# A 256-row transformer chain in split float32: x turned among the last products of the stage ahead, modulation sums and gate rows moved from TensorE to DMA and VectorE

## What is computed

```python
# block A, twice (l = 0, 1)
h = h + 0.5 * rms(swiglu(rms(h), w_in, w_out))        # stages 0 and 3, inner width 2816
m = even_mixer(rms(h)) if l == 0 else odd_mixer(rms(h))  # stage 1: attention and convolution; stage 4: GLA
h = h + rms(m)
h = h + 0.5 * rms(swiglu(rms(h), w_in, w_out))        # stages 2 and 5

# block B
mod = silu(c) @ w_ada + b_ada                         # 1024 x 6144, one row
shift1, scale1, gate1, shift2, scale2, gate2 = split(mod, 6)
y = rms(x, n1) * (1 + scale1) + shift1                # stage 6: projections, attention, retention
x = x + gate1 * (merged @ w_out)
y = rms(x, n2) * (1 + scale2) + shift2                # stage 7: swiglu
x = x + gate2 * ffn(y)
out = rms(x, final)
```

## Time and profile before

| | |
|---|---|
| runs | 1500.93, 1498.14, 1501.36 us; median 1500.93 |
| profiled execution | 1501.93 us, of which the span from first to last instruction is 1500.1 us |
| TensorE matmuls | 1452.5 us busy, 97% of the span, 6819 matmuls |
| TensorE weight load | 1195.0 us, 80% |
| VectorE, ScalarE, GpSimd | 938.8 us (63%), 723.6 us (48%), 167.0 us (11%) |
| DMA | 279.15 MB, mean 186 GB/s |
| mean granted clock of TensorE | 0.991 of 2.4 GHz |

### The profile page before, as it was taken

One profiled execution on the slowest core, in us unless ns is written; L12 is line 12 of the kernel. 1 busy time (PEld: TensorE's weight loads), 2 busy tenths in 40 slices (PEclk: granted clock), 3 DMA queues, 4 the chain that ended last, 5 costly groups with the idle time before them and its releaser, 6 DMA issues.

```text
span 1500.1 us, 17986 instructions
## 1 busy us (share of the span) xinstructions
PE 1452.5 (97%) x6819; PEld 1195.0 (80%) x6819; DVE 938.8 (63%) x1291; ACT 723.6 (48%) x1058; POOL 167.0 (11%) x260
## 2 busy tenths in 40 slices
PE   7999999999999999999899999999999999899998
PEld 6888878777888878888778788887877787688886
DVE  5666556677656476664667766654568566555553
ACT  5544355465444354443644544444555634444442
POOL 1700010000000010000153100000543110000000
PEclk9999999999999999999999999999999999999999
DMA  8766745127676576565533486653745344455551
GB/s 283 246 200 228 242 151 196 36 91 260 217 236 236 187 236 220 196 250 180 191 122 120 147 269 200 216 198 105 240 140 194 129 168 169 140 183 182 170 192 74
DMA packets 201717, 279.15 MB, mean 186 GB/s; under 512 B 8804, under 2 KB 126096, under 8 KB 201632
## 3 DMA queue, kind: packets, MB, share of 16 engines
q1 hardware_dynamic: 201376, 277.90, 55.0%
q10 hardware_dynamic: 256, 0.11, 0.0%
HBM read 276.93 MB, written 1.05 MB: 185 GB/s over the span
## 4 chain that ended last, share of the span: by engine, by line
PE 92%; ACT 3%; DVE 3%; issue 2%; POOL 0%; DMA 0%; ACTq 0%; DVEq 0%; POOLq 0%
PE ps L543 28%; PE ps L546 27%; PE ps L544 27%; PE ps L828 2%; PE ps L1062 1%; DVE wlo L464 1%; PE ps L710 1%; PE ps L1342 1%; ACT whi L455 1%; PE ps L495 1%; ACT xh L742 0%; ACT xtmp L1647 0%; DVE h L697 0%; PE ps L1013 0%; PE ps L986 0%
## 5 line engine op out<-in xcount | busy, mean ns | idle before, releaser
L464 DVE TENSOR_TENSOR wlo<-raw,whi 128x1024 fp32r<-128x1024 f32 (+2 forms) x474 | 565.3, 1222 | 199.9 <-ACT whi L455 199.6
L543 PE MATMUL ps<-whi,xh 128*128 128x512 f32 (+2 forms) x1440 | 573.1, 398 | 22.6 <-ACT xh L742 14.8
L544 PE MATMUL ps<-wlo,xh 128*128 128x512 f32 (+2 forms) x1440 | 559.2, 388 | 0.0
L546 PE MATMUL ps<-whi,xl 128*128 128x512 f32 (+2 forms) x1440 | 551.7, 389 | 0.0
L455 ACT ACTIVATE whi<-raw 128x1024 fp32r<-128x1024 f32 (+2 forms) x474 | 470.8, 1043 | 155.8 <-PE ps L546 152.1
L543 PEld LDWEIGHTS ps<-whi,xh 128*128 128x128 f32 x1440 | 273.4, 190 | 83.1 <-issue 22.9
L546 PEld LDWEIGHTS ps<-whi,xl 128*128 128x128 f32 x1440 | 273.0, 190 | 56.6
L544 PEld LDWEIGHTS ps<-wlo,xh 128*128 128x128 f32 x1440 | 273.5, 190 | 51.7 <-issue 0.2
L543 PE MATMUL ps<-whi,gh 128*128 128x512 f32 x440 | 173.0, 393 | 0.0
L544 PE MATMUL ps<-wlo,gh 128*128 128x512 f32 x440 | 171.3, 389 | 0.0
L546 PE MATMUL ps<-whi,gl 128*128 128x512 f32 x440 | 153.5, 389 | 0.0
(11 more groups left out here) (242 smaller groups left out, 967.6 us busy)
## 6 DMA issues: line engine op xcount, KB each, us to landing
raw<-in_ffn_w_in_dram SPq DMA_DIRECT2D x174, 512.0 KB, 4.9
raw<-in_ffn_w_out_dram SPq DMA_DIRECT2D x40, 1024.0 KB, 5.0
raw<-in_w_in_dram SPq DMA_DIRECT2D x26, 1024.0 KB, 4.9
adat<-in_w_ada_dram SPq DMA_DIRECT2D x96, 256.0 KB, 5.3
raw<-in_w_ffn_gate_dram SPq DMA_DIRECT2D x22, 512.0 KB, 3.9
raw<-in_w_ffn_up_dram SPq DMA_DIRECT2D x22, 512.0 KB, 5.1
raw<-in_hyb_w_in_dram SPq DMA_DIRECT2D x10, 1024.0 KB, 5.1
raw<-in_gla_w_in_dram SPq DMA_DIRECT2D x10, 1024.0 KB, 5.0
```

The costliest lines, as they stand in the source:

```text
L464: e.tensor_tensor(split_of(wlo, j), raw_of(j), split_of(whi, j).bitcast(F32), ALU.subtract).then_inc(*wlo_made.up(j))
L543: e.matmul(ps[:, 0:n], a, whi_of(j, k), start=first and k == 0, stop=False)
L544: last = e.matmul(ps[:, 0:n], a, wlo_of(j, k), start=False, stop=False)
L546: last = e.matmul(ps[:, 0:n], b, whi_of(j, k), start=False, stop=final and k == subs[j][2] - 1)
```

## The change

What it does, in parts:

1. `pe_down` takes `then`: the transposes of the next stage's tok 0 stand ahead of the last held product (ahead of the last two for stages 6 and 7). `LAG` becomes 6 in stages 4 and 6 and 7 in stage 5. With `late`, one sub-tile is popped less at the end.
2. `first_order` leads with six sub-tiles of tok 0 (seven in stages 6 and 7), and `late` stands ahead of the fifth (sixth).
3. ScalarE and VectorE have another order of splits at a stage's entry; `dve_residual` and `dve_ada_x` take `between`, a split put between their two steps.
4. K's turn moves from chunk 2 to the first step of chunk 3, Q's to the third; the levels' steps move earlier or later as in the list.
5. The modulation sums leave TensorE: SP stores `adaacc` to DRAM in four DMAs, in pieces of 32 floats, and reads it back in four, turned by blocks of 32; VectorE adds twice, turns 32x32 blocks, reduces and adds the bias. The adds of tiles move by two units.
6. The gate rows leave TensorE: SP writes eight columns of `modc` to DRAM and loads them as rows to all partitions.

```diff
-        LAG = {st: 4 if st == 1 else 5 for st in range(8)}
+        LAG = {0: 5, 1: 4, 2: 5, 3: 5, 4: 6, 5: 7, 6: 6, 7: 5}
...
-                if j == last_sub[u] and ada_tile(u, -1):
-                    ada_add(e, *ada_tile(u, -1))
+                if j == last_sub[u]:
+                    if u - 1 in ada_tiles:
+                        ada_add(e, *ada_tiles[u - 1])
+                    if u in ada_summed:
+                        ada_sum(e, ada_summed[u])
...
+        def ada_sum(e, c):
+            z = fold
+            e.wait_ge(*s_fold.at(c))
+            e.tensor_tensor(z[:, 0:256], z[:, 0:256], z[:, 256:512], ALU.add).then_inc(*ada_step.up(c, 0))
+            e.wait_ge(*ada_step.at(c, 0))
+            e.tensor_tensor(z[:, 0:P], z[:, 0:P], z[:, P:256], ALU.add).then_inc(*ada_step.up(c, 1))
+            e.wait_ge(*ada_step.at(c, 1))
+            e.transpose(z[:, 256:384], z[:, 0:P]).then_inc(*ada_step.up(c, 2))
+            e.wait_ge(*ada_step.at(c, 2))
+            e.tensor_reduce(modc[:, 4 * c:4 * c + 4], z[:, 256:384].rearrange("p (b n) -> p b n", b=4), AX.X, ALU.add
+                            ).then_inc(*ada_added.up(c, 8))
...
+        def load_ada(e, u):
+            if u in ada_tiles:
+                c, k = ada_tiles[u]
+                n = 8 * c + k
+                if n >= 2:
+                    e.wait_ge(*ada_added.at(*divmod(n - 2, 8)))
+                e.dma_start(adat[n % 2][:, :], ada_view[:, k, c * 512:(c + 1) * 512]).then_inc(*s_ada[n % 2].up(n))
+            if u in ada_sent:
+                c = ada_sent[u]
+                e.wait_ge(*ada_added.at(c, 7))
+                for b in range(4):
+                    e.dma_start(ada_out[c].rearrange("p (q b n) -> b p q n", q=4, b=4)[b],
+                                adaacc[:, b * P:(b + 1) * P].rearrange("p (q n) -> p q n", q=4)).then_inc(*s_sent.up(c))
+            if u in ada_read:
+                c = ada_read[u]
+                e.wait_ge(*s_sent.at(c))
+                e.wait_ge(*(mod_made.at(c - 1) if c else vec_made.at(1)))
+                for q in range(4):
+                    e.dma_start(fold[32 * q:32 * (q + 1), :].rearrange("p (r n) -> p r n", r=4),
+                                ada_out[c, :, q * P:(q + 1) * P].rearrange("(r p) n -> p r n", r=4)
+                                ).then_inc(*s_fold.up(c))
...
-            lead = {0: 4, 6: 6, 7: 6}.get(st, 5)
+            lead = {0: 4, 6: 7, 7: 7}.get(st, 6)
...
-                if (i, tok) == ((0, 1) if st >= 6 else (3, 0)):
+                if (i, tok) == ({0: 3, 6: 5, 7: 5}.get(st, 4), 0):
                     late()
...
-                if i < len(order) - lag and not late or len(held) > lag:
+                if i < len(order) - lag and not late or late and len(held) >= lag and i < len(order) - 1:
                     one(held.pop(0), 1)
-            for i in held:
+            for k, i in enumerate(held):
+                if then and k == len(held) - then[0]:
+                    then[1]()
                 one(i, 1)
...
+            return (2, lambda: pe_ada_x(e, st, 0)) if st >= 6 else (1, lambda: pe_enter(e, st, 0))
...
                 dve_residual(e, st - 1, 0)
+                split_lo(e, j0 + 4)
                 dve_enter(e, st, 0)
-                split_lo(e, j0 + 3)
-                dve_residual(e, st - 1, 1)
-                split_lo(e, j0 + 5)
+                dve_residual(e, st - 1, 1, lambda: split_lo(e, j0 + 5))
+                split_lo(e, j0 + 6)
...
+        GLA = [(1, "m"), (4, "a"), (3, "e"), (2, "m")]
+        for n in range(1, 9):
+            GLA += [(n, 0)] + [(n, 1)] * (n < 8)
+            GLA += [(k, s) for k, s in ((n + 4, "a"), (n + 3, "e"), (n + 2, "m")) if k < 9]
...
+            if i < 4:
+                return [["k", (1, "a")], [(2, "a")], ["q", (1, "e"), (3, "a")], [(0, 0), (0, 1), (2, "e")]][i]
+            return GLA[4 * (i - 4):4 * (i - 3)]
...
-            for tok in range(2):
-                if st == 6:
-                    dve_residual(e, 5, tok)
-                else:
-                    dve_residual_gate(e, 6, tok, 2)
+            if st == 6:
+                dve_residual(e, 5, 0)
+            else:
+                dve_residual_gate(e, 6, 0, 2)
+            split_lo(e, j0 + 2)
+            dve_ada_x(e, st, 0, lambda: split_lo(e, j0 + 3))
+            if st == 6:
+                dve_residual(e, 5, 1, lambda: split_lo(e, j0 + 4))
+            else:
+                dve_residual_gate(e, 6, 1, 2)
+            split_lo(e, j0 + 6)
+            dve_ada_x(e, st, 1, lambda: split_lo(e, j0 + 7))
...
+                if u in (U0[5] + 10, U0[6] + 8):
+                    i, which = (0, 2) if u < U0[6] else (1, 5)
+                    e.wait_ge(*mod_made.at(2 * which + 1))
+                    e.dma_start(gate_rows[i].rearrange("(b p) -> p b", p=P), modc[:, which * 8:which * 8 + 8],
+                                allow_slow_non_contiguous=True).then_inc(*s_gates.up(which))
+                if u == U0[6] + 10:
+                    load_row(e, "g2", gate_rows[0], D, [s_gates.at(2), f_scaled.at(5, 1, 1)])
+                if u == U0[7] + 4:
+                    load_row(e, "g5", gate_rows[1], D, [s_gates.at(5), gr_made.at(1, 1)])
```

More of the change, by code:

```diff
@@ L487, in pe_begin @@
                 pe_vectors(e, (1, 2))
-            if j in ada_sum_at:
-                c = ada_sum_at[j]
-                ps = tb.next(("ada", c), (mod_made, c))
-                for done in tb.freed:
-                    e.wait_ge(*done)
-                e.wait_ge(*ada_added.at(8 * c + 7))
-                for i in range(4):
-                    last = e.matmul(ps[:, i:i + 1], adaacc[:, i * P:(i + 1) * P], ones[:, 0:1], start=i == 0,
-                                    stop=True, skip_group_check=True)
-                last.then_inc(*ada_summed.up(c))
         def dve_begin(e, j):
@@ L607, in down_order, with pe_down @@
             return [(q, n) for k0, k1 in down_groups(nk) for n in range(2) for q in range(k0, k1, 2)]
-        def pe_down(e, key, j0, XH, XL, nk, new, readers, at=None, late=None, lag=3):
+        def pe_down(e, key, j0, XH, XL, nk, new, readers, at=None, late=None, lag=3, then=None):
             bank, freed = {}, {}
@@ L682, in act_f_squares, with dve_residual @@
                 act_squares(e, acc.of(("f", st), tok, n)[:, :], ("f", st, tok), n)
-        def dve_residual(e, st, tok):
+        def dve_residual(e, st, tok, between=None):
             row = rows[row_slot[st]]
@@ L851, in pe_ffn_in, with entry @@
                 pe_hid(e, st, c - 1)
+        def entry(e, st):
+            if st == 8:
+                return None
+            return (2, lambda: pe_ada_x(e, st, 0)) if st >= 6 else (1, lambda: pe_enter(e, st, 0))
         def pe_ffn(e, st):
@@ L865, in pe_ffn @@
             pe_down(e, ("f", st), j1, gh, gl, 22,
-                    lambda q, tok: (ghi_made.at(st, q // 2), glo_made.at(st, q // 2)), readers, at, lag=LAG[st])
+                    lambda q, tok: (ghi_made.at(st, q // 2), glo_made.at(st, q // 2)), readers, at, lag=LAG[st],
+                    then=entry(e, st + 1))
         def act_ffn(e, st, before):
@@ L1117, in pe_hyb @@
                     lambda q, tok: (o_hi.at(q + 1), o_lo.at(q + 1)) if tok == 0 else (),
-                    lambda tok, n: [(squares, ("f", 1, tok), n), (f_scaled, 1, tok, n)], norm, lag=LAG[1])
+                    lambda tok, n: [(squares, ("f", 1, tok), n), (f_scaled, 1, tok, n)], norm, lag=LAG[1],
+                    then=entry(e, 2))
         def act_hyb(e, before):
@@ L1345, in dve_gla_step @@
         def dve_gla_step(e, s):
+            if s == "k":
+                for b0 in (0, 2):
+                    e.wait_ge(*gla_turned.at("gk", b0))
+                    e.tensor_scalar(by_4(gKT)[:, b0:b0 + 2, :], turned(("gk",), b0), 1.0, None, ALU.mult
+                                    ).then_inc(*gla_qk.up("gk", b0))
+                return
             if s == "q":
@@ L1464, in pe_gla @@
                     lambda tok, n: [(squares, ("f", 4, tok), n), (f_scaled, 4, tok, n)], late=lambda: operand(1),
-                    lag=LAG[4])
+                    lag=LAG[4], then=entry(e, 5))
         def pe_gate_dot(e, hp):
@@ L1575, in dve_gla @@
                     dve_begin(e, GJ[c] + i)
-                    if c == 2 and i == 0:
-                        for b0 in (0, 2):
-                            e.wait_ge(*gla_turned.at("gk", b0))
-                            e.tensor_scalar(by_4(gKT)[:, b0:b0 + 2, :], turned(("gk",), b0), 1.0, None, ALU.mult
-                                            ).then_inc(*gla_qk.up("gk", b0))
                     if c == 2 and i == 3:
@@ L1662, in dve_ada_x @@
                                 ).then_inc(*x_scaled.up(st, tok, 0, b))
+            between()
             for q in range(2):
@@ L1709, in pool_ada_open @@
                 pool_rstd(e, ("h", st, tok))
[L1711 to L1734 removed]
         def dve_residual_gate(e, st, tok, which):
[L1737 removed]
+            name = "g2" if which == 2 else "g5"
```

(6 more changed lines are left out.)

137 lines of the change are left out of this document (41 added, 96 removed).

## The result

| | before | changed |
|---|---|---|
| median of the runs | 1501.14 us (1498.14 to 1502.52) | 1456.13 us (1455.35 to 1456.73) |
| ratio, 95% interval | | 0.9702, 0.9686 to 0.9719 |
| span of the profiled execution | 1500.1 us | 1454.9 us |
| TensorE busy, and idle in that span | 1452.5, 47.6 us | 1425.2, 29.7 us |

The change takes 45.0 us off, where 40 were forecast from the median (1461, range 1449 to 1479).

The account below looks back on a forecast made before the run. TensorE, busy 97% of the span, was taken to bound the kernel. Entries, GLA steps, sums and gate rows summed to 40.7 us off the profiled 1501.93 us, about 1461 us, range 1449 to 1479.

Parts of the forecast that it names:

- entries 0-1 to 4-5, with the wait for a sum's reader: Plain stage entries: turning x earlier removes waits, including 1.9 us for the sum's reader at 1-2; 9.3 us net.
- entries 5-6 and 6-7: Entries to the last two stages: more held products shorten waits and low-clock stretches; 4.4 and 6.8 us.
- GLA steps: GLA stage: moving K's and Q's turns and the exponentials saves 7.3 of 9.3 us, with 2 left at K.
- sums: Modulation sums: taking twelve times 0.79 us of passes off TensorE, with no gap around them, saves 9.5 us.
- gate rows: Two gate rows: taking 1.72 us each off TensorE saves 3.4 us; their transfers cost nothing.
- SP's wait: SP waits for adds, leaving two weight loads under way; two units need 10.7 us against 10.9 of products: 0.
- VectorE's new work: Five VectorE operations per sum, put at 2 us, lie beside products: 0 cost, range 0 to 3 us.
- (a): Token half 1's chain at entries moves but its gap stays, as do low clock and K's wait: 1474; chance 0.18.
- (b): Stages 0, 2, 3 and 5: two loads under way are too few; 1513 at 7.2 us landings; chance 0.05.
- (c): More goes than counted: no new waits at the last two entries or K, and further small ones: 1453; chance 0.14.
- (d): Splits set the pace, so TensorE's time freed from sums returns as low-half waits: 1474, up to 1490; chance 0.03.
- The rule on short stores: The sums' stores in 128 B pieces, under 512 B, may lengthen landings behind them, making (b) likelier; no size given.

Follow-up runs that it names:

- run 6: Changed kernel with each modulation tile's add two units earlier among VectorE's splits, so three weight loads are under way again; 1456.55 us, ratio 0.9714.
- run 9: Changed kernel without an edit, measured again on one chip beside two variants; 1456.59 us, ratio 0.9710.
- run 1: Changed kernel with modulation sums and gate rows back on TensorE, adds and SP's waits as before; entries and GLA steps stay changed; 1470.50 us, ratio 0.9799.
- run 10: Changed kernel with only the two gate rows back on TensorE, the twelve modulation sums staying on DMA and VectorE; 1459.26 us, ratio 0.9725.
- run 3: Changed kernel with all entries and the order of splits as before; sums, gate rows and GLA steps stay changed; 1483.84 us, ratio 0.9891.
- run 5: Changed kernel with the last two entries (5-6 and 6-7) and the order of splits there as before; 1466.21 us, ratio 0.9769.
- run 7: Changed kernel with all entries as before and the modulation tiles' adds early; 1480.34 us, ratio 0.9865.
- run 8: Changed kernel with each modulation tile also copied to DRAM, 96 more transfers on SP's queue that nothing waits for; 1476.18 us, ratio 0.9844.
- run 12: Changed kernel with each sum's tile stored in one transfer of 2 KB pieces and read back in sixteen short-piece reads; 1498.57 us, ratio 0.9984.

## Why the prediction was right, and where it was not

The sum of 40.7 us came out at 45.0. By its terms (measured: what taking that part back cost; the plain entries are what is left of 45.0):

| term | predicted | measured |
|---|---|---|
| entries 0-1 to 4-5, with the wait for a sum's reader | 9.3 | 13.6 |
| entries 5-6 and 6-7 | 11.2 | 10.1 |
| GLA steps | 7.3 | 6.9 |
| sums | 9.5 | 11.7 |
| gate rows | 3.4 | 2.7 |
| SP's wait | 0 | 0 (run 6) |
| VectorE's new work | 0 | not measured apart; it is in the sums' 11.7 |

**Plain entries: the term that was mis-sized.** The mechanism was right, the size was not: "That covers the 1.10 us five times: 5.5 us", and 0.32 and 0.41 us for token half 1. These are idle times as the view prints them, from the modelled end of one matmul to the start of the next. What TensorE loses runs from start to start. Around token half 0 that is 2.13 - 0.79 = 1.34 us, 0.24 more than the 1.10. Around token half 1 it is 1.71 - 0.79 = 0.92 behind the transposes, and in front of them:

```profile
207.51 0.61 PE L546 MATMUL ps<-whi,xl 128*128 128x512 f32 x2
```

Two products 0.23 us apart from 207.51 on, so the last starts at 207.74, and the transposes at 208.44 are 0.47 later than 0.23 would give. Together 1.39 us where the two brackets say 0.73. Five of 1.34, three of 1.39, one of 1.1 (entry 3-4, where the first part is only 0.17) and a low half's wait behind two of them, 0.40 each, make 12.8; the sum's reader at entry 1-2 adds 2.1. That is 14.9. The wait that is new in stage 0 takes 1.4 off again, a term that the prediction does not have, and one of 0.2 stays at entry 1-2; 13.3 is left, where 13.6 was measured. The prediction's 1.2 us for x coming late behind VectorE's splits did not occur: before the first products of stages 1 to 5 TensorE's timeline has one wait, 0.23 us at entry 1-2. That this term, which did not come, and the new waits nearly cancel is luck.

**Sums.** The same error in small. The chain gives eight passes 0.79 us; from start to start the timeline of before has this around one of them:

```profile
99.39 0.94 PE L495 MATMUL ps<-ones,adaacc 128*128 128x1 f32 x8
100.20 0.49 PE L543 MATMUL ps<-whi,xh 128*128 128x512 f32 x1
100.52 0.40 PE L544 MATMUL ps<-wlo,xh 128*128 128x512 f32 x1
```

0.81 us to the next product, and that one holds the next back by 0.32 in place of 0.23: 0.90, twelve times 10.8, where 11.7 was measured. The gate rows by the same reading are 1.72 each, as predicted, and 1.4 as measured. The prediction put their transfers at nothing. The wait of 0.66 us in stage 6 (0.22 in run 9) goes with them: TensorE has it in ten of the eleven kernels with these transfers and in none of the three without (before, 1 and 10). It can be part of the difference of 0.7, but that is not shown, since the runs of 9 and 10 spread over more.

**The last two entries and GLA** came out within 1.1 us. The waits are about where they were put: 0.84 and 0.71 us at entry 5-6 (1.3 forecast), 1.14 ahead of token half 0 at entry 6-7 (1.2 forecast) and 1.5 in three at token half 1 (0.9), 1.2 at K (up to 2). The low clock went with the long waits: run 3, with the old entries, has it at the last two again, as the windows below show (stretch, us, busy per engine, granted clock). It does not follow each such wait: run 5 has the four waits of 2.2 us, and the granted clock behind them is 0.51 once (1013.6 to 1017.0 us) and 1.00 three times, so its 10.1 us hold less of it than the 11.2 counted on.

```profile
1029.80:1032.00 2.20, 2.20 (x6) 1.67 (x6) 2.20 (x4) 0.75 (x4) 0.94 (x3) 0.51 0.00 0
1282.40:1285.00 2.60, 2.60 (x7) 2.04 (x8) 2.60 (x4) 1.24 (x2) 0.00 (x0) 0.50 0.00 0
```

**SP's wait** cost nothing, as forecast, but the reason given ("It just holds") holds only with the entries changed: with the old ones it costs 3.5 us (run 7). With a quarter more bytes the kernel loses 20 (run 8); what SP's wait has in that was not tried.

**The rivals.** (a), that the chain of token half 1 would be late in the plain entries, has no wait for it at all. (b), two loads too few, did not happen; runs 8 and 12 show that it was nearer than its chance of 0.05 lets one think, and that issues in one line on SP's queue lead there as well as long landings do. (c) named the right direction for a wrong reason: the waits at the last entries and at K stand; the additional gain is in the terms above. (d) is refuted by run 1: the sums' time came off in full and more. Of the signs that were named, one failed: TensorE's idleness before the first products of stages 6 and 7 was to stay under 0.5 us, and is 0.71 and 0.59 at two of them.

**The rule on short stores.** The trace shows stores in pieces of 128 B landing after 4.7 us for 64 KB, and reads of 64 KB in pieces of 512 B after 2.5. By the Trainium skill, "DMA: Bandwidth & Descriptors", Specifications, transfers in pieces under 512 B are done as read-modify-write and do not reach the full rate. Run 12 does not bear it out as a cost of this kernel for the sums' stores: a store of 256 KB in pieces of 2 KB landed after 5.7 us and the ffn_w_out loads after 6.5, no sooner than with the short ones (6.0). It is no clean test of the rate, as SP's issues moved too. Where short pieces do go with late landings is the store of a gate row, in pieces of 4 B (last section).

## What to carry to other kernels

Price a gap from the start of the last instruction ahead of it to the start of the next one behind it, and against the same pair where nothing waits; the idle time in brackets is short by 0.1 to 0.5 us each here, which over some two dozen small places comes to some 5.7 us, against the 4.3 by which the sum was short. Work that is taken off the bounding engine onto a DMA queue costs issues there: count them against the time in which the queue must also issue the loads, since a queue that mostly waits can still be one load late. Look also at what lands behind a small store in tiny pieces, and not only at when the store itself is needed. And take a part back with the other parts in place as well as alone: here the two readings differ by 3 to 4 us (14.4 and 11.0 for the sums and gate rows, 27.7 and 23.7 for the entries), since late splits and a short supply only hurt together.

## What the runs showed of the hardware

**Weight loads land late around a store in pieces of 4 bytes.** SP writes eight columns of `modc` to DRAM as a gate row of 4 KB, one float per piece. The transfers issued from 1031 to 1039 us (KB each, median us to landing) in the changed kernel, and behind the dots in run 10, which has the gate rows on TensorE and the same loads at this place:

```profile
raw<-in_w_in_dram SPq DMA_DIRECT2D x3, 1024.0 KB, 13.2
gate_rows<-modc SPq DMA_DIRECT2D x1, 4.0 KB, 15.0
...
raw<-in_w_in_dram SPq DMA_DIRECT2D x3, 1024.0 KB, 5.9
```

The other gate row, at 866.60 us, has two loads behind it that landed after 11.0 and 12.7 us; in run 10 the two at this place took 5.0 and 6.7. From 20 us on, no weight load of the three kernels without this store (before, 1 and 10) takes 10 us; each of the eleven kernels with it has loads of 11 to 15 us there. A row load of 512 KB is under way at 1039 us too, but at the first store it is not. In the changed kernel ScalarE waits 6.7 us for one of these loads, and TensorE has 0.66 us of waiting behind it; the 1.93 us of run 3 and the 6.54 of run 12 also follow such a store. The prediction counted only when the rows are read. A variant with the store in longer pieces was not tried.

**GpSimd is slow beside VectorE's splits.** At entry 6-7 the same two instructions of one column stand once beside a gap and once beside three splits:

```profile
1253.63 0.19 POOL L689 TENSOR_SCALAR st<-st 128x1 f32<-128x1 f32 x1
1253.90 0.55 POOL L691 TENSOR_TENSOR st<-st,mhalf 128x1 f32<-128x1 f32 x1
...
1262.62 3.48 DVE L468 TENSOR_TENSOR wlo<-raw,whi 128x1024 fp32r<-128x1024 f32 x3
...
1263.97 1.05 POOL L689 TENSOR_SCALAR st<-st 128x1 f32<-128x1 f32 x1
1265.10 1.41 POOL L691 TENSOR_TENSOR st<-st,mhalf 128x1 f32<-128x1 f32 x1
```

0.74 us became 2.46, and the rstd that they make is what the 0.49 us wait at 1267.41 hangs on. The kernel has each of the two 46 times, with medians of 0.19 and 0.55 us; these are the longest. What holds them up was not tried.

**Issues take unequal time.** Sixteen reads of 16 KB in pieces of 128 B took 10.95 us to issue in run 12, 0.68 each; in the changed kernel a read of 64 KB in pieces of 512 B took 0.43 (median), a store of 64 KB in pieces of 128 B 0.68, and a weight load some 0.5.
